# Order of the 512-column and the 256-column matmul in alternate weight tiles of a decoder block

## The chip, the cores and the metric

The kernel runs on one core of one Trainium2 chip, as one program of 20,150 profiled instructions. The metric is the device time of one execution in microseconds. The core has five engines with their own instruction streams: TensorE (PE in the profile; its weight loads are shown apart, as PEld), VectorE (DVE), ScalarE (ACT), GpSimd (POOL) and SyncE (SP), which issues most of the DMAs.

## What is computed

One layer of a decoder for 256 tokens of width 2048, in float32: a mixer with 16 heads of three kinds, cross attention with four heads over a memory of 256 tokens, and an MLP of width 8192, each with a residual and an RMS norm.

```python
h = rms_norm(x, g_mix)
qkv = h @ w_in                          # 2048 x 6144
merged = concat(rms_norm(moba(q, k, v)), rms_norm(stick_breaking(q, k, v)),
                rms_norm(dilated_mixture(q, k, v)))
x = x + merged @ w_out                  # 1536 x 2048
x = x + cross_attention(rms_norm(x), rms_norm(mem), w_cq, w_ckv, w_co)
u = rms_norm(x) @ w_up                  # 2048 x 8192
x = x + square(relu(u)) @ w_down        # 8192 x 2048
return rms_norm(x, g_final)
```

## The kernel before

Every product of the reference with a weight matrix is done in two parts, high and low. A float32 operand is split into a `float32r` value (`high`) and the rest (`low`), and a product is the sum of three: high by high, high by low, and low by high. ScalarE makes the high part of the weights (`w_high`, a copy, line 364), VectorE the low part (`w_low`, a subtraction, line 673). The activations stand in `part_a` or `part_b` as `[128, tile, 2, 256]`: for each tile of 128 rows of the contraction the high part and behind it the low part, for 256 tokens.

The weights come in jobs of 1 MB (`staged`, four buffers). A job has 16 weight tiles of 128 x 128. `w_high` and `w_low` each hold two jobs. TensorE takes a job in two halves of 8 tiles (`half_job`, line 1004). Ahead of a half it waits until VectorE has counted `low_ready` for it, and with the last matmul of a half it counts `half_done`, on which ScalarE waits before it splits the same half of the job after next into the same place.

Most jobs are *wide*. For a wide tile TensorE issues two matmuls. The one here called W has the high weights as its stationary operand and all 512 columns of the tile (high and low activations together) as its moving operand, and writes all 512 columns of a PSUM bank. The one called L has the low weights and the 256 high columns, and adds into the bank's first 256 columns. After the job the bank's two halves are added: VectorE and ScalarE do that while TensorE is in the next jobs (there are four banks). The first tile of a bank has to begin with W, since only W covers the whole bank and clears it (line 1020); the other tiles have L first (line 1021) and W second (line 1023).

The wide jobs are: 12 jobs of the q and k projections for the stick-breaking heads (one job for one bank of 16 tiles), 8 jobs of the output projection (two banks of 8 tiles each), 4 jobs of the cross attention's query, and the 128 jobs of the MLP. The MLP goes in four quarters, each with 16 jobs `up` and 16 jobs `down`. The `down` jobs read `part_b`, which holds the quarter's 16 tiles of squared activations. Before tiles 0, 8, 12 and 15 of its first job, `down` waits for `hid_low`, which VectorE counts when such a tile is ready (line 961).

The rest of the jobs use other forms: the value projections with matmuls of 512 columns only (lines 1066 to 1068), and the rotary heads, the memory keys, part of the output projection and the cross output with three matmuls of 256 columns for a tile (lines 1025 to 1027). All run in the order in which they are written; no scheduler moves anything.

Of the kernel before, what the change touches and what calls it, by code (L numbers as in the profile page):

```python
# [86 lines left out]
def build(nc, x_in, mem_in, wqk_in, wv_in, wmk_in, wmv_in, wbc_in, woa_in, wcq_in, wco_in,  # L87
# [4 lines left out]
    with ExitStack() as ctx:  # L92
# [908 lines left out]
        def _(pe):  # L1001
            mm = nc.tensor.matmul

            def half_job(off, job, half, out, part, tiles, count=8, total=KT, place=0, wide=True,
                         slot=lambda kt: kt, waits={}):

                pe.wait_ge(low_ready, off(2) + (2 * job + half + 1))
                for n in range(count):  # L1010
                    if n in waits:
                        pe.wait_ge(*waits[n])
                    kt = tiles + n
                    cols = slice(half * HALF + (place + n) * P, half * HALF + (place + n + 1) * P)
                    high, low = w_high[:, job % 2, cols], w_low[:, job % 2, cols]
                    first, last_tile = kt == 0, kt == total - 1
                    if wide:
                        both = part[:, slot(kt), :, :].rearrange("p a n -> p (a n)")
                        if first:
                            mm(out[:, :], high, both, start=True, stop=False)  # L1020
                        last = mm(out[:, 0:T], low, part[:, slot(kt), 0, :], start=False, stop=False)  # L1021
                        if not first:
                            last = mm(out[:, :], high, both, start=False, stop=last_tile)  # L1023
                    else:
                        mm(out[:, 0:T], high, part[:, slot(kt), 0, :], start=first, stop=False)  # L1025
                        mm(out[:, 0:T], high, part[:, slot(kt), 1, :], start=False, stop=False)  # L1026
                        last = mm(out[:, 0:T], low, part[:, slot(kt), 0, :], start=False, stop=last_tile)  # L1027
                return last

            def job_of(off, job, n_out, part, ready=None, wide=True, slot=lambda kt: kt):  # L1030

                pe.wait_ge(taken, off(1) + (n_out + 1))
                for half in range(2):
                    waits = {}
                    if ready is not None:

                        waits = ({0: (ready, 12), 4: (ready, 14), 6: (ready, KT)} if half
                                 else {0: (ready, 8)})
                    half_job(off, job, half, bank[job % 4], part, 8 * half, wide=wide,
                             slot=slot, waits=waits).then_inc(half_done, 1)  # L1040

            def short_jobs(job, n_out, part, at, waits={}):

                for s in range(4):
                    for half in range(2):
                        for t in (2 * half, 2 * half + 1):
                            pe.wait_ge(taken, n_out + 4 * s + t + 1)
                            last = half_job(none, job + s, half, bank[t], part, 0, 4, 4,
                                            place=4 * (t % 2), wide=False, slot=lambda kt: at + kt,
                                            waits={} if s or t else waits)  # L1050
                        last.then_inc(half_done, 1)
# [95 lines left out]
            with pe.Fori(0, HEADS_A // 2) as i:  # L1147
                for s in range(4):
                    job_of(by(i), JOB_A + s, OUT_A + s, part_a, wide=False)
                    if s == 0:  # L1150
                        pe.wait_ge(held_ready, i * 6 + (3 * 4 + 6))
                        pe.wait_ge(o_taken, i + (1 + HEADS_B))
                        for g in range(3):
# [3 lines left out]
                                      start=True, stop=True)  # L1157
# [42 lines left out]
            for s in range(8):  # L1200
                for half in range(2):
                    t = 2 * s + half
                    pe.wait_ge(taken, OUT_BC + t + 1)
                    pe.wait_ge(merged_low, 8)
                    half_job(none, JOB_BC + s, half, bank[t % 4], part_a, 0, 8, 8).then_inc(half_done, 1)
                if s < 4:
                    group_a(1, s)
                if s == 5:
                    norm_sum(N_A, extra[3])
# [164 lines left out]
```

## Time and profile before

| what | value |
|---|---|
| time, median of 3 runs | 1224.55 us (1224.54 to 1224.73) |
| span of the profiled execution | 1222.6 us |
| PE busy | 1205.0 us (99%), 7164 matmuls |
| PE weight loads busy | 1063.4 us (87%) |
| VectorE busy | 797.6 us (65%) |
| ScalarE busy | 605.1 us (49%) |
| GpSimd busy | 172.4 us (14%) |
| DMA | 224.25 MB, 183 GB/s over the span |
| chain of work that ended last | PE 92%, DVE 5%, the rest 3% |

Matmuls are pipelined, so that one starts long before the record of the one ahead ends. The duration in a matmul's row is therefore not what it costs. Its cost in a stream is the distance from its start to the start of the next. The start times in the timeline have a resolution of 0.01 us, so that a price of a few nanoseconds is read over many matmuls, or over several places of the same kind.

### The profile page before, as it was taken

Reading aid. Unit: us, or ns where it says so; the run is one execution under the profiler, and the core shown is the slowest. Engines: PE = TensorE matmul, PEld = TensorE weight load, DVE = VectorE, ACT = ScalarE, POOL = GpSimd, SP = SyncE. Lnnn points to the kernel's source line nnn. Section 1 sums busy time; section 2 is a strip of 40 time slices with the busy share of each in tenths; the row PEclk is TensorE's granted clock in tenths of the full one; section 3 lists DMA queues with packets and bytes.
Section 4 is the critical chain, followed back from the end, with each engine's and each line's share of the span. In section 5 each row is a group of like instructions: output and inputs, shape, how many; then the busy total and the mean of one; then the engine's idle time right before and its main releaser. Section 6 shows DMA issues by size and latency. Waiting matters only on the chain.

```text
span 1222.6 us, 20150 instructions
## 1 busy us (share of the span) xinstructions
PE 1205.0 (99%) x7164; PEld 1063.4 (87%) x7164; DVE 797.6 (65%) x1085; ACT 605.1 (49%) x897; POOL 172.4 (14%) x176
## 2 busy tenths in 40 slices
PE   8999999999999999999999999999999999999996
PEld 6888899999989889888888888888888888888885
DVE  8658766786668858666555666655666555666554
ACT  6345445555645656555433555333555333555442
POOL 8206500030323405000000000000000000000342
PEclk9999999999999999999999999999999999999998
DMA  9674543443644544455554455545555555455531
GB/s 357 213 269 174 201 177 138 144 166 137 242 172 169 177 153 155 151 196 186 196 199 174 172 191 187 206 172 197 172 180 183 197 197 177 172 186 196 200 138 69
DMA packets 33011, 224.25 MB, mean 183 GB/s; under 512 B 3793, under 2 KB 4177, under 8 KB 7121
## 3 DMA queue, kind: packets, MB, share of 16 engines
q1 hardware_dynamic: 32256, 220.22, 50.3%
q10 hardware_dynamic: 720, 3.59, 0.8%
q8 instruction: 21, 0.34, 0.1%
q14 instruction: 14, 0.11, 0.0%
HBM read 221.69 MB, written 2.10 MB: 183 GB/s over the span
## 4 chain that ended last, share of the span: by engine, by line
PE 92%; DVE 5%; ACT 1%; POOL 1%; issue 1%; DMA 0%; DVEq 0%; SPq 0%; ACTq 0%; POOLq 0%
PE bank L1023 43%; PE bank L1021 23%; PE bank L1025 4%; PE bank L1027 4%; PE bank L1026 4%; PE bank L1020 3%; PE bank L1066 2%; PE bank L1067 2%; PE bank L1068 2%; DVE w_low L673 2%; DVE part_a L718 1%; DVE part_a L883 1%; PE extra L1083 1%; POOL acc L302 0%; ACT w_high L364 0%
## 5 line engine op out<-in xcount | busy, mean ns | idle before, releaser
L673 DVE TENSOR_TENSOR w_low<-staged,w_high 128x1024 fp32r<-128x1024 f32 x407 | 508.5, 1264 | 215.6 <-ACT w_high L364 210.7
L364 ACT ACTIVATE w_high<-staged 128x1024 fp32r<-128x1024 f32 x400 | 415.0, 1054 | 338.2 <-PE bank L1023 244.8
L1023 PE MATMUL bank<-part_a,w_high 128*128 128x512 f32 x1312 | 467.7, 398 | 0.0
L1021 PE MATMUL bank<-part_a,w_low 128*128 128x256 f32 x1408 | 379.6, 281 | 0.0
L1023 PE MATMUL bank<-part_b,w_high 128*128 128x512 f32 x960 | 342.4, 399 | 0.0
L1023 PEld LDWEIGHTS bank<-part_a,w_high 128*128 128x128 f32 x1312 | 246.5, 188 | 56.8
L1021 PE MATMUL bank<-part_b,w_low 128*128 128x256 f32 x1024 | 277.2, 281 | 0.0
L1021 PEld LDWEIGHTS bank<-part_a,w_low 128*128 128x128 f32 x1408 | 266.0, 189 | 7.9
L1023 PEld LDWEIGHTS bank<-part_b,w_high 128*128 128x128 f32 x960 | 180.4, 188 | 42.0
L1021 PEld LDWEIGHTS bank<-part_b,w_low 128*128 128x128 f32 x1024 | 193.5, 189 | 5.5
L293 POOL TENSOR_TENSOR squares<-x 128x256 f32<-128x256 f32 (+1 forms) x31 | 35.0, 1130 | 683.3 <-DVE x L971 678.7
L1025 PE MATMUL bank<-part_a,w_high 128*128 128x256 f32 x384 | 110.1, 287 | 0.1
L1027 PE MATMUL bank<-part_a,w_low 128*128 128x256 f32 x384 | 108.7, 283 | 0.0
L1026 PE MATMUL bank<-part_a,w_high 128*128 128x256 f32 x384 | 108.6, 283 | 0.0
L961 DVE TENSOR_TENSOR part_b<-spare,part_b 128x256 f32 x64 | 27.2, 425 | 79.8 <-ACT part_b L633 79.8
L1025 PEld LDWEIGHTS bank<-part_a,w_high 128*128 128x128 f32 x384 | 73.7, 192 | 0.5 <-POOL part_a L307 0.4
L1026 PEld LDWEIGHTS bank<-part_a,w_high 128*128 128x128 f32 x384 | 73.6, 192 | 0.1
L1027 PEld LDWEIGHTS bank<-part_a,w_low 128*128 128x128 f32 x384 | 73.6, 192 | 0.0
L628 ACT ACTIVATE spare<-bank 128x256 f32<-128x256 f32 x64 | 24.5, 383 | 85.9 <-PE bank L1023 85.9
L295 POOL TENSOR_TENSOR acc<-acc,squares 128x256 f32<-128x256 f32 x59 | 59.7, 1011 | 4.6
L631 ACT ACTIVATE spare<-spare 128x256 f32<-128x256 f32 x64 | 26.7, 418 | 65.5 <-DVE spare L957 65.5
L969 DVE TENSOR_TENSOR x<-x,bank 128x256 f32 (+1 forms) x64 | 26.9, 421 | 46.1 <-PE bank L1023 45.9
(153 smaller groups left out, 1162.2 us busy)
## 6 DMA issues: line engine op xcount, KB each, us to landing
staged<-in_wup SPq DMA_DIRECT2D x64, 1024.0 KB, 4.8
staged<-in_wdown SPq DMA_DIRECT2D x64, 1024.0 KB, 4.7
staged<-in_wqk SPq DMA_DIRECT2D x32, 1024.0 KB, 4.8
staged<-in_wv SPq DMA_DIRECT2D x12, 1024.0 KB, 4.9
staged<-in_wbc SPq DMA_DIRECT2D x8, 1024.0 KB, 5.0
staged<-in_wmk SPq DMA_DIRECT2D x4, 1024.0 KB, 4.8
staged<-in_woa SPq DMA_DIRECT2D x4, 1024.0 KB, 4.8
staged<-in_wcq SPq DMA_DIRECT2D x4, 1024.0 KB, 4.9
```

The costliest lines, as they stand in the source:

```text
L293: nc.gpsimd.tensor_tensor(squares[:, 0, :], tile, tile, ALU.mult).then_inc(sq_made, 1)
L295: nc.gpsimd.tensor_tensor(acc[:, :], acc[:, :], squares[:, 0, :], ALU.add).then_inc(acc_made, 1)
L364: nc.scalar.activation(w_high[:, job % 2, cols], staged[:, job % 4, cols], ACT.Copy).then_inc(high_ready, 1)
L673: tt(w_low[:, job % 2, cols], staged[:, job % 4, cols], f32(w_high[:, job % 2, cols]), ALU.subtract).then_inc(low_ready, 1)
L961: tt(part_b[:, i * 4 + s, 1, :], spare[:, 1, :], f32(part_b[:, i * 4 + s, 0, :]), ALU.subtract).then_inc(hid_low, 1)
L969: tt(x[:, i * 4 + s, :], x[:, i * 4 + s, :], bank[s][:, 0:T], ALU.add).then_inc(x_wide, 1)
L1020: mm(out[:, :], high, both, start=True, stop=False)
L1021: last = mm(out[:, 0:T], low, part[:, slot(kt), 0, :], start=False, stop=False)
L1023: last = mm(out[:, :], high, both, start=False, stop=last_tile)
L1025: mm(out[:, 0:T], high, part[:, slot(kt), 0, :], start=first, stop=False)
L1026: mm(out[:, 0:T], high, part[:, slot(kt), 1, :], start=False, stop=False)
L1027: last = mm(out[:, 0:T], low, part[:, slot(kt), 0, :], start=False, stop=last_tile)
```

## The change

In wide tiles the order of the two matmuls now depends on the tile's number: tiles with an even number have W first and L second, tiles with an odd number L first and W second. Before, tile 0 had W first and all others L first. The operands, the number of matmuls and the waits stay as they are. The flag that clears the bank is on W of tile 0 as before.

```diff
                     if wide:
                         both = part[:, slot(kt), :, :].rearrange("p a n -> p (a n)")
-                        if first:
-                            mm(out[:, :], high, both, start=True, stop=False)
+                        if kt % 2 == 0:
+                            mm(out[:, :], high, both, start=first, stop=False)
                         last = mm(out[:, 0:T], low, part[:, slot(kt), 0, :], start=False, stop=False)
-                        if not first:
+                        if kt % 2:
                             last = mm(out[:, :], high, both, start=False, stop=last_tile)
```

The first place is on TensorE, at the start of a 16-tile job of the q and k projections: `bank1` is the job's PSUM bank, L1020 and L1023 are the two lines of W, L1021 is L. Before, from the first tile on:

```order
L1009 REGISTER_ALU
L1020 MATMUL bank1<-part_a,w_high 128x512
L1021 MATMUL bank1<-part_a,w_low 128x256 x2
L1023 MATMUL bank1<-part_a,w_high 128x512
L1021 MATMUL bank1<-part_a,w_low 128x256
L1023 MATMUL bank1<-part_a,w_high 128x512
```

With the change:

```order
L1009 REGISTER_ALU
L1020 MATMUL bank1<-part_a,w_high 128x512
L1021 MATMUL bank1<-part_a,w_low 128x256 x2
L1023 MATMUL bank1<-part_a,w_high 128x512
L1020 MATMUL bank1<-part_a,w_high 128x512
L1021 MATMUL bank1<-part_a,w_low 128x256 x2
L1023 MATMUL bank1<-part_a,w_high 128x512
```

The four matmuls that already opened the job (W, L, L, W) now repeat for each two tiles, where L and W had alternated.

The second place is on TensorE too, in the output projection with its banks of 8 tiles, behind six transposes of the attention. Before:

```order
L1094 MATMUL extra<-square,values 128x128 x6
L1020 MATMUL bank<-part_a,w_high 128x512
L1021 MATMUL bank<-part_a,w_low 128x256 x2
L1023 MATMUL bank<-part_a,w_high 128x512
L1021 MATMUL bank<-part_a,w_low 128x256
L1023 MATMUL bank<-part_a,w_high 128x512
```

With the change:

```order
L1094 MATMUL extra<-square,values 128x128 x6
L1020 MATMUL bank<-part_a,w_high 128x512
L1021 MATMUL bank<-part_a,w_low 128x256 x2
L1023 MATMUL bank<-part_a,w_high 128x512
L1020 MATMUL bank<-part_a,w_high 128x512
L1021 MATMUL bank<-part_a,w_low 128x256 x2
```

Here, too, the first two tiles stay, and the third one's W has moved ahead of its L. On the other engines no instruction moves.

## Rows read from the trace of the kernel before

**Rows 1.** The page: the span, and the TensorE clock granted in 40 slices.

```profile
span 1222.6 us, 20150 instructions
...
PEclk9999999999999999999999999999999999999998
```

**Rows 2.** Waits of PE: line, waited for, us in total, times, longest.

```profile
PE bank L1066 <- DVE w_low L673: 2.8, 6, 1.6
PE extra L1075 <- POOL acc L302: 1.9, 2, 1.1
```

**Rows 3.** Busy time by stretch: us, then us and count of each engine, clock, DMA.

```profile
101.00:168.00 67.00, 67.00 (x381) 58.21 (x381) 53.78 (x62) 35.58 (x51) 35.26 (x33) 1.00 0.49 179
...
500.00:1211.00 711.00, 711.00 (x4032) 617.60 (x4031) 434.91 (x567) 335.38 (x455) 33.63 (x30) 1.00 0.51 180
```

**Rows 4.** Timeline of PE from one up job's start to the next: start, duration.

```profile
702.72 0.40 PE L1023 MATMUL bank<-part_a,w_high 128*128 128x512 f32 x1
702.96 0.39 PE L1020 MATMUL bank<-part_a,w_high 128*128 128x512 f32 x1
703.18 0.40 PE L1021 MATMUL bank<-part_a,w_low 128*128 128x256 f32 x2
703.42 0.40 PE L1023 MATMUL bank<-part_a,w_high 128*128 128x512 f32 x1
703.65 0.28 PE L1021 MATMUL bank<-part_a,w_low 128*128 128x256 f32 x1
703.77 0.40 PE L1023 MATMUL bank<-part_a,w_high 128*128 128x512 f32 x1
704.01 0.28 PE L1021 MATMUL bank<-part_a,w_low 128*128 128x256 f32 x1
...
708.60 0.39 PE L1020 MATMUL bank<-part_a,w_high 128*128 128x512 f32 x1
...
709.30 0.28 PE L1021 MATMUL bank<-part_a,w_low 128*128 128x256 f32 x1
```

**Rows 5.** The same timeline from 703.5 us, where only the second L is left.

```profile
703.30 0.28 PE L1021 MATMUL bank<-part_a,w_low 128*128 128x256 f32 x1
```

**Rows 6.** PE in the value projections, first and last of 19 matmuls.

```profile
61.76 0.39 PE L1068 MATMUL bank<-w_high,part_a 128*128 128x512 f32 x1
...
65.84 0.39 PE L1068 MATMUL bank<-w_high,part_a 128*128 128x512 f32 x1
```

**Rows 7.** PE in jobs of three 256-column matmuls, first and last of 36.

```profile
388.73 0.28 PE L1026 MATMUL bank<-part_a,w_high 128*128 128x256 f32 x1
...
392.93 0.28 PE L1025 MATMUL bank<-part_a,w_high 128*128 128x256 f32 x1
```

**Rows 8.** PE at the start of the first down stage and of the second up stage.

```profile
578.73 0.39 PE L1020 MATMUL bank<-part_b,w_high 128*128 128x512 f32 x1
...
579.42 0.28 PE L1021 MATMUL bank<-part_b,w_low 128*128 128x256 f32 x1
...
669.08 0.39 PE L1020 MATMUL bank<-part_a,w_high 128*128 128x512 f32 x1
```

**Rows 9.** The lines L1020 and L1021 alone: count, duration min/median/max, first and last start.

```profile
L1020 PE MATMUL bank<-part_a,w_high x96: 389/389/585, 100.9 to 1115.2; 128*128 128x512 f32 x96
...
L1020 PE MATMUL bank<-part_b,w_high x64: 389/389/389, 578.7 to 1205.5; 128*128 128x512 f32 x64
...
L1021 PE MATMUL bank<-part_a,w_low x1408: 274/281/285, 101.2 to 1120.5; 128*128 128x256 f32 x176
...
L1021 PE MATMUL bank<-part_b,w_low x1024: 277/281/284, 579.0 to 1210.8; 128*128 128x256 f32 x171
```

**Rows 10.** Timeline: last hidden tile ready on DVE, and its first use by PE.

```profile
581.56 0.42 DVE L961 TENSOR_TENSOR part_b<-spare,part_b 128x256 f32 x1 [1.26 <-ACT part_b L633]
...
584.02 0.28 PE L1021 MATMUL bank<-part_b,w_low 128*128 128x256 f32 x1
```

**Rows 11.** Timeline around the output projection's end: ACT, POOL and PE.

```profile
376.16 1.06 ACT L364 ACTIVATE w_high<-staged 128x1024 fp32r<-128x1024 f32 x1 [2.24 <-PE bank L1023]
...
382.19 2.31 POOL L307 TENSOR_TENSOR part_a<-spare,part_a 128x256 fp32r<-128x256 f32 x2 [0.81 <-ACT part_a L503]
...
384.55 0.39 PE L1025 MATMUL bank<-part_a,w_high 128*128 128x256 f32 x1
```

## The prediction, made before the changed kernel had run

> **What bounds the kernel now.** I read the page's head first, then the waits of PE, then the busy times by stretch, and last the starts in PE's timeline one by one. The granted clock is at the full 2.4 GHz from the first slice to the last [rows 1], so nothing here is about the clock. PE waits for other engines for a few us in all: 2.8 us for low weights in the first 32 us, 1.9 us for GpSimd's sums before two norms [rows 2]. In the stretches of the wide jobs it never stands still: 67.00 us busy in 67, and 711.00 in 711 through the MLP, where VectorE is busy 434.91 and ScalarE 335.38 [rows 3]. So in these stretches the time is the number of matmuls times the distance between their starts. The busy share can't show whether such a distance is as short as it could be; the starts can.
>
> **What a pair of matmuls costs, by its neighbours.** I call the 512-column matmul W and the 256-column one L. In an up job [rows 4] the first four starts are W 702.96, L 703.18, L 703.30 [rows 5], W 703.42, and the next tile's L is at 703.65. From there L and W alternate for 14 tiles until the next job's W at 708.60: 4.95 us / 14 = 353.6 ns for a tile, 707 ns for two. One such tile shows the parts: L 703.65 to W 703.77 is 0.12, W 703.77 to L 704.01 is 0.24. The first two tiles of the job, with the same two W and two L but in the order W L L W, take 703.65 - 702.96 = 0.69 us. The same distance is 0.70 one job later [rows 4] and 579.42 - 578.73 = 0.69 in a down job [rows 8]. As a cross-check, a whole job takes (669.08 - 578.73) / 16 = 5.647 us [rows 8]; less 14 x 0.3536 = 4.950 this leaves 0.697. So W L L W costs 0.690 to 0.697 where L W L W costs 0.707.
>
> Two other stages tell the same without mixing lengths. Where every matmul has 512 columns, 18 distances take 65.84 - 61.76 = 4.08 us, or 226.7 ns each [rows 6]. Where every matmul has 256, 35 distances take 392.93 - 388.73 = 4.20 us, or 120.0 ns each [rows 7]. Two of each make 2 x (226.7 + 120.0) = 693 ns. That is the price of W L L W, and not that of the alternation, which costs 14 ns more. An order with equal neighbours thus costs what the pure streams cost, and each return from W to L in the alternation is dearer: a W that follows an L takes 0.236 or so, one that follows a W takes 0.22 to 0.23 (702.96 to 703.18). Why that is I can't read from the records, and the sum doesn't need it.
>
> **The change part by part.** It removes no matmul and adds none. It turns each two tiles that read L W L W into W L L W, except the first two of each bank, which have that order already. How many are there? L1021 counts 1408 + 1024 = 2432 wide tiles, L1020 counts 96 + 64 = 160 banks [rows 9]. Of the 160, 144 banks have 16 tiles (12 + 4 + 128 jobs) and 16 have 8: 144 x 16 + 16 x 8 = 2432, which agrees. Two tiles of each bank are as before, so 144 x 7 + 16 x 3 = 1056 groups of four matmuls change their order.
>
> The saving for a group is 707.2 - 693 = 14.2 ns by the pure streams, and 707.2 - 692.5 = 14.7 by the mean of the job starts at 0.69, 0.69 and 0.70. One thing in the new order has no row: in it the second W of a group is followed by another W, where at the job start it is followed by an L. The nearest row is the last W of a job, followed by the next job's W: 702.96 - 702.72 = 0.24, no dearer than the alternation's. I take 14.5 ns. 1056 x 14.5 = 15.3 us.
>
> What of this is not on the path? At three places a chain on other engines ends the stage, and TensorE gets to the wait earlier without gaining. At the end of the output projection, PE goes on at 384.55, right as GpSimd's second subtraction ends (382.19 + 2.31 = 384.50), a chain that begins with ScalarE's split at 376.16 [rows 11]. In these 8.4 us stand some 9 changed groups, whose 9 x 14.5 = 0.13 us is lost. The two waits for GpSimd's sums [rows 2] come each behind one wide job of 7 groups, the first of the cross query and the first of the MLP: 2 x 7 x 14.5 ns = 0.2 us lost. That leaves 15.3 - 0.3 = 15.0 us.
>
> What would be late next? The weights: ScalarE and VectorE have to split each job in 5.54 us where they had 5.65. VectorE is busy 434.91 / 711 = 61% of the MLP and 53.78 / 67 = 80% of the q and k stage [rows 3]. 2% less time makes that 62% and 82%, and PE waits for neither now. The hidden activations: the last tile of a quarter is ready at 581.56 + 0.42 = 581.98, and down uses it first at 584.02 [rows 10], with 2.04 us to spare. Seven groups in between shorten that by 0.1. The banks, and the count at a half's end, stand where they stood: the last matmul of each half is W of an odd tile before and after. The loads follow VectorE's splits and run at half the DMA engines' share [rows 3]. So I cost all of these at nothing.
>
> The profiled execution: 1222.6 - 15.0 = 1207.6 us. The median of the runs shown stands 1.95 us above the span, which the change doesn't touch: **1209.5 us**.
>
> **The bounds.** A W behind a pair of L and ahead of a W has no row, so I bound it from both sides. At best it takes the 226.7 ns of the pure stream, where the job start has it at about 0.233 (703.42 to 703.65): 1056 x 6 ns = 6 us less, 1203.5. At worst it takes the 0.236 of the alternation: 1056 x 3 ns = 3 us more, 1212.7. I hold the upper end, with a us for reading errors of 1 ns in a group, at 1214, and the lower at 1205, since the row nearest to the case (0.233) speaks against the whole of the gain.
>
> **Rivals.** First, *no change*: the short distance belongs to the start of a bank. There W clears the bank in place of adding to it, and it goes to another bank than the W before. Inside a bank W would then cost 0.236 whatever stands ahead of it. What remains is a few ns at most: 1224.5, and not below 1222. For it speaks that my row of a W behind a W in mixed jobs is always at such a start. Against it: in rows 6 nearly every matmul adds (line 1066 clears only at tile 0), three in a row go to the same bank, and the mean is still 226.7. I give it 6 in 100. The Trainium skill (TensorE: Matmul & The Clock Gate, section Back-to-back issue gap) has a rule that leads to the same end: the distance of warm matmuls is their columns / 2.4 plus some 2.5 ns, with no word on the neighbours. By that rule W costs 216 and L 109 ns in either order, and this change gives nothing. The trace does not agree with it: 226.7 and 120.0 in the pure streams, and 0.24 for W in the alternation. What the rule lacks is just what is at issue.
>
> Second, *half of it*: the cheap W (0.22 against 0.24) needs a new bank, but the two L next to each other, with their common 0.24 for the two (703.18 to 703.42), and the W behind them keep their price. Then a group costs about 0.701 in place of 0.693, the saving is 6 ns, and the time 1224.55 - 1056 x 6 ns = 1218.2. For and against it stand the same rows. I give it 5 in 100.
>
> Third, *slower*: two W in one bank disturb each other. The second W starts to add to column 0 of the bank 0.23 us after the first, while the record of the first lasts 0.39 to 0.40 us [rows 4]. In the old order an L stands between two W of a bank, except where the bank changes. If the second had to wait for the first one's record to end, it would cost 0.17 us in each of 1056 groups, 180 us in all. It decides from 14.5 ns a group. Against it: rows 6 have three such matmuls in a row in one bank at 226.7 ns, and the two L at the job's start overlap in the same way. A weak form, of 30 ns a group, would give 1224.5 + 1056 x 15.5 ns = 1241. 2 in 100.
>
> **How the numbers follow.** The forecast has 87 in 100, no change 6, half of it 5, slower 2. The range for 8 in 10 is that of the forecast alone, 1205 to 1214. About 0.2% (2.4 us) is what a measurement of this kernel can tell from no change. Faster by more: 87 + 5 and a little of the rest, 0.92. Within: 0.06. Slower: 0.02.
>
> **What would show it.** In the changed kernel's timeline two tiles in the middle of an up job should take 0.69 us where now they take 0.707, a whole job 5.54 in place of 5.65, and the stages with matmuls of one length should stay at 226.7 and 120.0 ns. The sum is right if the span falls by 15 us, about 13 of them between the MLP's begin and its end. The waits of PE should show no new line in the MLP. Wrong would be: W behind W inside a bank at 0.24 (first or second rival) or more (third), or a new wait for VectorE's low weights.

## The result and the profile after

The changed kernel takes 1214.47 us (median of 4 runs, 1214.26 to 1214.81), the kernel before 1224.58 beside it. The ratio is 0.9917, with a 95% interval of 0.9904 to 0.9931. So it is faster by 10.1 us, where 15.0 were forecast: the direction is right, and the time lies half a microsecond above the stated range.

The page of the changed kernel, its head and the granted clock, against [rows 1], and the waits of PE, against [rows 2]:

```profile
span 1212.5 us, 20150 instructions
...
PEclk9999999999999999999999999999999999999999
```

```profile
PE bank L1066 <- DVE w_low L673: 2.6, 5, 1.6
PE extra L1075 <- POOL acc L302: 2.0, 2, 1.1
```

The busy times by stretch, against [rows 3] (stretch, then us and count of PE, weight loads, VectorE, ScalarE, GpSimd; clock; DMA share and GB/s):

```profile
101.00:168.00 67.00, 67.00 (x387) 58.53 (x388) 55.09 (x64) 35.91 (x51) 35.16 (x33) 1.00 0.51 182
500.00:1200.00 700.00, 700.00 (x4021) 611.09 (x4020) 434.34 (x566) 334.50 (x454) 33.58 (x30) 1.00 0.51 183
```

The clock is at its upper level as before and PE is still busy without a gap. The waits are those of before but for one: in the first 20 us, ahead of every changed instruction, PE also waits 1.1 us for low weights of another line (L724), 0.9 us more for low weights in all. Nothing new bounds the wide stages, and the whole gain lies in the distances of the starts. The timeline of PE at the start of the first down stage, and at the start of the second up stage 16 jobs later, against [rows 8]:

```profile
576.86 0.39 PE L1020 MATMUL bank<-part_b,w_high 128*128 128x512 f32 x1
577.09 0.40 PE L1021 MATMUL bank<-part_b,w_low 128*128 128x256 f32 x2
577.33 0.40 PE L1023 MATMUL bank<-part_b,w_high 128*128 128x512 f32 x1
577.56 0.40 PE L1020 MATMUL bank<-part_b,w_high 128*128 128x512 f32 x1
577.79 0.39 PE L1021 MATMUL bank<-part_b,w_low 128*128 128x256 f32 x2
578.02 0.40 PE L1023 MATMUL bank<-part_b,w_high 128*128 128x512 f32 x1
578.26 0.39 PE L1020 MATMUL bank<-part_b,w_high 128*128 128x512 f32 x1
...
666.03 0.39 PE L1020 MATMUL bank<-part_a,w_high 128*128 128x512 f32 x1
```

A job takes (666.03 - 576.86) / 16 = 5.573 us, where it took 5.647 and 5.54 was forecast. Two tiles take (578.26 - 576.86) / 2 = 0.70 us, not 0.69. From here on I give distances in nanoseconds, taken from the start times in the trace. They repeat to a nanosecond or two. L118 is an L whose follower starts 118 ns after it. The two kernels in the middle of an up job read:

```
before   L118 W241  L120 W236  L113 W232 | L118 W241  L120 W236  L113 W232 | ...    1060 for 3 tiles, 353.3 each
after    W231 L113  L120 W233  W236 L116  L112 W233 | W231 L112 ...                 1393.3 for 4 tiles, 348.3 each
```

Where the 10.1 us lie can be read by comparing when each stage begins in the two traces. The middle column is the prediction's sum, split by its own counts of groups (84, 48, 28 and 896, at 14.5 ns) and its own losses:

| stretch | gain in the sum, us | gain measured, us |
|---|---|---|
| up to the first wide job | 0 | -0.32 |
| q and k | 1.22 | 0.88 |
| output projection | 0.57 | 0.08 |
| cross query | 0.30 | 0.12 |
| MLP | 12.89 | 9.31 (127 jobs x 73.3 ns) |

The first wide job begins 0.32 us later in the changed kernel. That shift is there by 16 us, where no instruction differs, and goes from run to run: in the traces of this study that job begins between 100.84 and 101.58 us.

### The profile page after: what moved, and what is told of

It is laid out like the page before. It is cut to its first block, busy times and chain, and to the rows that moved or that the text cites. A ratio compares the mean times of both kernels' runs of the same rounds, so it can differ in the third digit from the quotient of the medians.

```text
span 1212.5 us, 20150 instructions
## 1 busy us (share of the span) xinstructions
PE 1193.7 (98%) x7164; PEld 1057.0 (87%) x7164; DVE 797.9 (66%) x1085; ACT 605.0 (50%) x897; POOL 172.4 (14%) x176
## 4 chain that ended last, share of the span: by engine, by line
PE 92%; DVE 5%; ACT 1%; POOL 1%; issue 1%; DMA 0%; DVEq 0%; SPq 0%; ACTq 0%; POOLq 0%
PE bank L1023 23%; PE bank L1020 23%; PE bank L1021 23%; PE bank L1025 4%; PE bank L1027 4%; PE bank L1026 4%; PE bank L1066 3%; PE bank L1067 2%; PE bank L1068 2%; DVE w_low L673 2%; DVE part_a L718 1%; DVE part_a L883 1%; PE extra L1083 1%; DMA staged<-in_wv 0%; POOL acc L302 0%
## 5 line engine op out<-in xcount | busy, mean ns | idle before, releaser
L1021 PEld LDWEIGHTS bank<-part_a,w_low 128*128 128x128 f32 x1408 | 264.7, 188 | 61.9
L1020 PE MATMUL bank<-part_a,w_high 128*128 128x512 f32 x704 | 279.7, 397 | 0.0
L1023 PE MATMUL bank<-part_a,w_high 128*128 128x512 f32 x704 | 278.5, 396 | 0.0
L1021 PE MATMUL bank<-part_a,w_low 128*128 128x256 f32 x1408 | 276.6, 278 | 0.0
L1021 PEld LDWEIGHTS bank<-part_b,w_low 128*128 128x128 f32 x1024 | 192.5, 188 | 45.3
L1023 PE MATMUL bank<-part_b,w_high 128*128 128x512 f32 x512 | 202.5, 396 | 0.0
L1020 PE MATMUL bank<-part_b,w_high 128*128 128x512 f32 x512 | 202.3, 395 | 0.0
L1021 PE MATMUL bank<-part_b,w_low 128*128 128x256 f32 x1024 | 201.1, 278 | 0.0
L1020 PEld LDWEIGHTS bank<-part_a,w_high 128*128 128x128 f32 x704 | 133.7, 190 | 0.2
L1023 PEld LDWEIGHTS bank<-part_a,w_high 128*128 128x128 f32 x704 | 131.9, 187 | 0.0
L1027 PE MATMUL bank<-part_a,w_low 128*128 128x256 f32 x384 | 108.7, 283 | 0.0
L1020 PEld LDWEIGHTS bank<-part_b,w_high 128*128 128x128 f32 x512 | 97.2, 190 | 0.0
L1023 PEld LDWEIGHTS bank<-part_b,w_high 128*128 128x128 f32 x512 | 95.9, 187 | 0.0
L1025 PEld LDWEIGHTS bank<-part_a,w_high 128*128 128x128 f32 x384 | 73.7, 192 | 0.5 <-POOL part_a L307 0.4
L1026 PEld LDWEIGHTS bank<-part_a,w_high 128*128 128x128 f32 x384 | 73.7, 192 | 0.1
```

The source lines that it names most:

```text
L1020: mm(out[:, :], high, both, start=first, stop=False)
```

## The experiments

The diffs in this section are abridged, but for the first; a comment in them stands for lines that are left out. Jobs are timed from the first matmul of one to the first of the next.

### Alternation from the first tile to the last

My first theory (A) was the prediction's: each matmul has a price by its neighbours. The rival (B) came from a second look at the trace of before. There the alternation L W does not have one price. In the output projection seven of the 16 banks of 8 tiles read 233, 117, 231, 112 from their third tile on, that is 346.7 ns for a tile, and two more go at this price in their later tiles; so does one of the cross query's four jobs. Two banks in a row, in steps and by their first matmuls:

```
before, 345.6   W236 L116 L112 W233  L117 W231 L112 W233  L117 W231 L113 W232  L118 W231 ...   346.7 a tile
before, 348.3   W230 L114 L119 W233  L118 W241 L120 W235  L114 W232 L118 W241  L120 W235 ...   353.3 a tile
```

```profile
345.56 0.40 PE L1020 MATMUL bank<-part_a,w_high 128*128 128x512 f32 x1
348.34 0.39 PE L1020 MATMUL bank<-part_a,w_high 128*128 128x512 f32 x1
351.16 0.40 PE L1020 MATMUL bank<-part_a,w_high 128*128 128x512 f32 x1
```

The first bank takes 2.78 us, the second, with the same matmuls in the same order, 2.82. So there are two steady rhythms, which I call the fast one (346.7 ns a tile) and the slow one (353.3). The kernel of this run never has two of a kind side by side:

```diff
-                        if first:
-                            mm(out[:, :], high, both, start=True, stop=False)
-                        last = mm(out[:, 0:T], low, part[:, slot(kt), 0, :], start=False, stop=False)
-                        if not first:
-                            last = mm(out[:, :], high, both, start=False, stop=last_tile)
+                        mm(out[:, :], high, both, start=first, stop=False)
+                        last = mm(out[:, 0:T], low, part[:, slot(kt), 0, :], start=False, stop=last_tile)
```

> In every wide tile W (512 columns) stands ahead of L (256), so that the two alternate from the first tile to the last and nowhere two of a kind meet. Theory A (the price of a matmul hangs on its neighbours: each change between lengths costs some ns, two of a kind side by side save it): 353.7 ns for a tile everywhere, no cheap start of a job, 5.65 us for a job or a little more, about 1225.5 us. Theory B (the starts fall into one of two steady rhythms, 346.7 or 353.3 ns for a tile of alternating matmuls, both seen in the kernel before; which one holds is set by the steps at a job's start, and the two L side by side there bring the slow one back): with no such pair the rhythm of the first job stays, 5.547 us a job and about 1210.5 us if it is the fast one, 5.653 us a job and 1225.5 if it is the slow one, and it may change only where another stage comes in between.

Measured: ten runs, and they form two groups with nothing between. Four lie at 1211.81, 1212.29, 1212.35 and 1212.37 us, six from 1225.04 to 1226.14 (a mean ratio of 0.9970, 0.9936 to 1.0005, says nothing of either). The trace was of the first kind. The first matmul of its first down stage and of its second up stage:

```profile
577.97 0.39 PE L1019 MATMUL bank<-part_b,w_high 128*128 128x512 f32 x1
...
666.71 0.39 PE L1019 MATMUL bank<-part_a,w_high 128*128 128x512 f32 x1
```

(666.71 - 577.97) / 16 = 5.546 us a job, the pure price (832 x 6.667 ns). In the same trace the q and k stage has the slow rhythm; two matmuls in it that are ten jobs apart:

```profile
107.29 0.40 PE L1019 MATMUL bank<-part_a,w_high 128*128 128x512 f32 x1
...
163.82 0.40 PE L1019 MATMUL bank<-part_a,w_high 128*128 128x512 f32 x1
```

(163.82 - 107.29) / 10 = 5.653 us a job. Theory A, with one price for one order, can explain neither the two groups nor the two stages. The distance between the groups, 13.3 us by their means, is near the 127 jobs x 106.7 ns = 13.5 us that the rhythms ask for.

> The kernel with W ahead of L in every wide tile once more, for a second trace of it: its ten times fell into two groups, four at 1211.8 to 1212.4 us and six at 1225.0 to 1226.1, and the trace was taken of the first kind (5546.5 ns for each MLP job). Rhythm theory: a run of the other kind has 5653 ns for each MLP job from the first to the last, never a mixture; the difference of 106.7 ns x 127 = 13.5 us is that of the two groups. If it is of the first kind again the MLP jobs read 5547. Against it: prices in between, or a change in the middle of the MLP.

Measured: 1212.15 us in one run, MLP jobs of 5547 ns again, the q and k stage slow again. No trace shows this kernel in its other group; a slow MLP with this order is shown by the last kernel below. Both traces have the first MLP job in the slow rhythm and all later ones in the fast. Between the first and the second PE waits for GpSimd's sum for the norm, 1.08 us in both, here in the first one's trace:

```profile
494.23 0.70 PE L1072 MATMUL extra<-acc,square 128*128 128x256 f32 x2 [1.08 <-POOL acc L302]
```

Behind that pause the rhythm is another. So a pause can be where one run parts from the next; that it was so in the runs at 1225 us is not shown.

### Longer stretches of one kind

```diff
-                for n in range(count):
+                for n in range(0, count, 4):      # tiles n to n + 3
+                    # W of the four tiles, then their L; in every second group L first
```

> Each half of 8 wide tiles has four W, eight L and four W, so that the lengths change twice in a half where the changed kernel has them change four times and the kernel before some 15 times. The waits for a tile's activations stand ahead of its group of four. Theory A (changes of length cost): the changed kernel's excess over the pure streams (5.573 - 5.547 = 0.027 us a job) halves, 5.56 us a job, about 1212.5 us. Theory B (rhythms): long runs pin each length to its pure price, 226.7 and 120.0 ns, 5.547 us a job, about 1210.7 us; a price above the changed kernel's would speak against both.

Measured: 1216.09 us (4 runs, ratio 0.9930, 0.9911 to 0.9946), 5587 ns a job. Both theories expected less than the changed kernel's 5573, and both missed. (The changed kernel changes lengths eight times in a half, not four as the expectation has it; theory A should have said 5553, and missed by more.) The steps show a price that neither had:

```
runs of four   L120 L120 L120  W233 W236 W228 W233 W231 W226 W227 W227  L113 L119 L120 L120 ...
```

Behind a stretch of L the next five W cost 233, 236, 228, 233 and 231 where the pure price is 226.7, together 27 ns more. The first L behind a stretch of W costs 113 in place of 120. A return costs 20 ns in all, there are two in a job, and 5547 + 40 = 5587.

> W x8, L x8 in the first half of a job, L x8, W x8 in the second, so that a job has one stretch of 16 W (across the job's border) and one of 16 L. Per-change theory as the runs of four read: a change from a long stretch of L to W costs 20 ns over the pure prices, spread over the next five W, and one from W to L nothing: 5546.7 + 20 = 5567 ns a job, 0.9 us less than the changed kernel over 144 jobs, about 1213.6, plus the waits: the activations' counts now stand ahead of a whole half, and the first down job of a quarter asks for tile 15 some 0.4 us before it is ready (4 x 0.4 = 1.8 us) and the first jobs after a norm likewise: about 1215.5 us. If the length of a stretch doesn't matter, 5587 a job as with the runs of four and 1218.

Measured: 5567 ns a job, as worked out from that price, but 1217.19 us (4 runs, 0.9939, 0.9923 to 0.9956). The waits of PE in this kernel, in its line numbers (L1020 is L):

```profile
PE bank L1020 <- DVE part_a L883: 2.9, 2, 1.5
...
PE bank L1020 <- DVE part_b L961: 1.7, 4, 0.5
```

The four waits for the hidden activations cost 1.7 us, where 1.8 were expected; those behind the two norms cost 2.9, more than I had put down. So a price that was read from one kernel's steps foretold another's job to the nanosecond, though not its waits.

### Which side the dear steps come from

```diff
-                        last = mm(out[:, 0:T], low, part[:, slot(kt), 0, :], start=False, stop=False)
+                        last = mm(low_out[:, 0:T], low, part[:, slot(kt), 0, :],   # extra[2] in the MLP
+                                  start=first, stop=last_tile)
```

> The order of the kernel before, but in the MLP's 128 jobs L writes into another PSUM bank (extra2) than W, so that no two neighbours touch the same bank; the low part is left out of the sums, which leaves the number of matmuls and the work of the other engines as they are. If the dear steps come from two matmuls that add into the same columns one right behind the other, a tile falls from 353.7 to 346.7 ns, the job to 5.55 us, about 1212 us. If they come from the sides of weights and moving columns, or from a rhythm of the starts, nothing changes: 5.647 us a job and 1224.5 us.

Measured: 1224.66 us in one run, 5647 ns a job, and the steps of the kernel before (L117 W241 L120 W236 L113 W233). Two neighbours that add into the same bank are not the cause.

```diff
-                        last = mm(out[:, 0:T], low, part[:, slot(kt), 0, :], start=False, stop=False)
+                        last = mm(out[:, 0:2 * T], low, both, start=False, stop=False)   # MLP only
```

> In the MLP's 128 jobs L moves 512 columns too, so that the low weights meet the low activations as well (work that the kernel before leaves out), in the order of the kernel before. If the pure price that the prediction took from the value projections holds where the weights are the stationary operand, every step is 226.7 ns, a tile 453.3 and a job 7253 ns: 128 x 1607 ns = 205.6 us more, about 1430 us. If W costs more in this place (233, as most W of the changed kernel), a job is near 7460 ns and the time 1456.

Measured: 1428.81 us, in one run. The first matmul of the first down stage and of the second up stage:

```profile
603.22 0.39 PE L1020 MATMUL bank<-part_b,w_high 128*128 128x512 f32 x1
...
719.27 0.39 PE L1020 MATMUL bank<-part_a,w_high 128*128 128x512 f32 x1
```

(719.27 - 603.22) / 16 = 7.253 us a job. The pure price of [rows 6] holds here as well, 32 x 226.7 ns. The steps there are 225 to 228 ns throughout. This stream of one length shows no rhythm; the extra nanoseconds came with the mixture.

### Where the two places stand that have two of a kind

```diff
-                        if first:
+                        if kt < heads:          # heads: 16, 7, 8, 5 in up, 16, 1, 4, 11 in down
                             mm(out[:, :], high, both, start=first, stop=False)
                         last = mm(out[:, 0:T], low, part[:, slot(kt), 0, :], start=False, stop=False)
-                        if not first:
+                        if kt >= heads:
                             last = mm(out[:, :], high, both, start=False, stop=last_tile)
```

> In the MLP the first n tiles of a job have W first and the rest L first, with n = 16, 7, 8, 5 for the four jobs of an up loop and 16, 1, 4, 11 for those of a down loop (the kernel before has n = 1 everywhere). Each job with n under 16 has one place with two L side by side and one with two W. Rhythm theory: between such places the distance is 346.7 or 353.3 ns for a tile and nothing else, the places are where it changes, and which one follows depends on how many tiles stand between, so that jobs of one loop differ among themselves by up to 100 ns but repeat from loop to loop. Neighbour theory: all jobs with n under 16 cost 5647 as before, those with n = 16 5660, whatever n is.

Measured: 1220.22 us, in one run. From the second job of the first down stage on, with n = 1, 4, 11, 16, the jobs cost 5647, 5646, 5631, 5554, then 5551, 5651, 5631, 5554 ns, and so on in that loop. The job with n = 1, the order of the kernel before, costs 5647 the first time and 5551 the three times after, and so in each of the four down stages. Its first matmul and that of the next job, the first time and the second:

```profile
584.52 0.40 PE L1020 MATMUL bank<-part_b,w_high 128*128 128x512 f32 x1
590.17 0.39 PE L1020 MATMUL bank<-part_b,w_high 128*128 128x512 f32 x1
...
607.00 0.39 PE L1020 MATMUL bank<-part_b,w_high 128*128 128x512 f32 x1
612.55 0.39 PE L1020 MATMUL bank<-part_b,w_high 128*128 128x512 f32 x1
```

5.65 us and 5.55: one order, two prices, by what ran before it. In the up loop n = 16, 7, 8, 5 cost 5644, 5647, 5631 and 5558; the neighbour theory had 5660 and 5647.

> As the kernel before, but each job of 16 tiles has its first n tiles with W first and the rest with L first, with n = 4 in the 12 jobs of the q and k stage, 2 in the up jobs and 8 in the down jobs (the kernel before has n = 1). The matmuls and the number of places with two of a kind side by side (two in a job) are those of the kernel before. Neighbour theory: each n costs 5647 ns a job, 1224.5 us. Rhythm theory: the price of n is its own, between 5551 (fast between the two places) and 5650 (slow), the same from job to job once it has settled. In the traces so far the fast rhythm has a period of two tiles and went over to the slow one where two W met after an odd count of tiles with L first; with an even n that count is even (12, 14 or 8), so that fast may follow fast: then 5.55 us in the MLP and about 1211 us.

> The same with n = 6 in the q and k stage, 12 in the up jobs and 7 in the down jobs. Neighbour theory: 5647 ns everywhere, 1224.5 us. Rhythm theory: again a price for each n between 5551 and 5650; if even counts let the fast rhythm stay, n = 6 and 12 are near 5551 and n = 7 is not, and a quarter of the MLP (16 up, 16 down) costs some 1.5 us less than before.

Measured, in one run each: 1218.43 us with n = 4, 2, 8 and 1222.74 with n = 6, 12, 7. The neighbour theory's 5647 for every n is wrong. But the other expectation holds only in part: most n settle at a price of their own, n = 2 and 8 never settle at one, n = 12 has two, and the even-odd rule is wrong:

| tiles with W first | ns a job, once settled |
|---|---|
| 1 (kernel before) | 5647 |
| 2, 8 | 5560 and 5633 in turn |
| 4 | 5647 |
| 6 | 5593 |
| 7 (down jobs) | 5647 |
| 12 | 5627, from the second quarter on 5633 |

What these traces gave was a list of steps. The fast rhythm comes in two forms, 230, 117 in each tile or 233, 117, 231, 112 in two. The slow one goes 241, 120, 236, 113, 233, 117 in three tiles (5650, 5650 and 5660 ns for 16 tiles, in turn). Two of a kind side by side lead from one to the other, and which way depends on the step at which they meet. Two L behind a slow "W233 L117" lead on as 121, 238, 117, 236, 116, 224, 117, 234, 117, 241. Two W behind a slow 241 lead to 238 and then to 230, 117 for good.

### One job that decides 126

If that list is right, an order of matmuls in one job has to set the time of all that follow. The MLP alternates throughout with W first; the other stages have the changed kernel's order; only the second of the 128 MLP jobs differs, and differently in the two kernels:

```diff
+            def up(off, s, ready=None, order="WL" * 8):       # of a half; down has it too
             for s in range(4):
-                up(none, s, x2_low if s == 0 else None)
+                # fast: first half "W" * 8 + "L" * 8, second "WL" + "LW" * 5 + "WL" * 2
+                # slow: first half "W" * 8 + "L" * 8, second "WL" * 8
+                up(none, s, x2_low if s == 0 else None, one_job if s == 1 else "WL" * 8)
```

> All MLP jobs alternate with W first (W L W L), as in the kernel of the first run, and the other stages have the changed kernel's order; only the MLP's second job differs: W x8, L x8, then W L, five tiles with L first and two with W first. By the steps of the traces so far the eight L wipe out what was before, the alternation behind them is slow and reads 234, 117 (one tile), two L side by side bring 121, 238, 117, 236, 116, 224, 117, 234, 117, 241, and two W side by side right behind the 241 bring 238 and then the fast rhythm of 230 and 117. Rhythm theory: each of the 126 MLP jobs behind it costs 5547 ns in every run, 26.7 ns less than in the changed kernel, 3.4 us in all: 1211.1 us, with no second group of times at 1225. If the steps hang on something else than the order of the matmuls, the times fall into two groups again, or lie at 1224.5.

> The same kernel, but the MLP's second job has W x8, L x8 and then eight tiles with W first, without the two places that lead to the fast rhythm. The same matmuls in the same order in the 126 jobs behind it. Rhythm theory: the slow rhythm holds from there to the end in every run, 5653 ns a job, 126 x 106.7 ns = 13.4 us more than its neighbour: 1224.5 us. Neighbour theory, or any in which a job's cost comes from its own order: both kernels within 0.2 us of each other.

Measured: 1210.95 us with the fast job (4 runs, 1210.65 to 1211.05; ratio 0.9890, 0.9873 to 0.9906) and 1224.63 with the slow one (10 runs, 1224.06 to 1224.88; ratio 0.9999, 0.9990 to 1.0009). Neither has a second group of times. The fast one's timeline at that job's end, with the two W side by side at 497.63:

```profile
497.17 0.28 PE L1023 MATMUL bank<-part_a,w_low 128*128 128x256 f32 x1
497.28 0.40 PE L1021 MATMUL bank<-part_a,w_high 128*128 128x512 f32 x1
497.52 0.28 PE L1023 MATMUL bank<-part_a,w_low 128*128 128x256 f32 x1
497.63 0.64 PE L1021 MATMUL bank<-part_a,w_high 128*128 128x512 f32 x2
498.11 0.28 PE L1023 MATMUL bank<-part_a,w_low 128*128 128x256 f32 x1
498.23 0.39 PE L1021 MATMUL bank<-part_a,w_high 128*128 128x512 f32 x1
498.46 0.28 PE L1023 MATMUL bank<-part_a,w_low 128*128 128x256 f32 x1
498.57 0.39 PE L1021 MATMUL bank<-part_a,w_high 128*128 128x512 f32 x1
```

The times in these rows are too coarse to tell 346.7 from 353.3; the steps tell them apart. From the two L side by side on they are:

```
L117 L121 W238 L117 W236 L116 W224 L118 W233 L117 W241 W238 L116 W230 L117 | W230 L117 W230 L116 ...
```

These are the steps that had been expected, to the nanosecond or two to which they repeat, and behind the two W (241 and 238, together the 0.48 us from 497.63 to 498.11) comes the fast rhythm, and it stays. In the slow kernel the second half of that job reads W233 L118 W241 L120 W236 L113 W232 L118, and this stays too. The same two starts, 16 jobs apart, in the fast kernel and in the slow one:

```profile
576.23 0.39 PE L1021 MATMUL bank<-part_b,w_high 128*128 128x512 f32 x1
...
664.98 0.39 PE L1021 MATMUL bank<-part_a,w_high 128*128 128x512 f32 x1
```

```profile
578.41 0.40 PE L1021 MATMUL bank<-part_b,w_high 128*128 128x512 f32 x1
...
668.87 0.40 PE L1021 MATMUL bank<-part_a,w_high 128*128 128x512 f32 x1
```

88.75 / 16 = 5.547 us against 90.46 / 16 = 5.654. The matmuls between these starts, their order, their operands and their waits are the same in both. Of the 13.7 us between the two kernels, 13.4 lie in the 126 jobs behind the one that differs, up to 700 us after it. This settles that the price is not in an order alone but in the rhythm that a stream is in, and that the rhythm can be set. The fast kernel is 3.5 us faster than the changed one, and the fastest of this study.

## Why the prediction missed

- **What bounds the kernel, and what would be late next.** Right. PE's starts were the bound before and after, VectorE, the hidden tiles and the loads never became one, and no new wait appeared in the MLP.
- **The count of 1056 groups.** Right as a count. But the groups of the output projection were not all of the dear kind: about half of its banks were already in the fast rhythm. In a slow bank the change saves some 29 ns (2816 to 2787), in a fast one it costs 9 (2777 to 2786). The stage gave 0.08 us, where 0.57 were in the sum. I had read the alternation's price in the MLP alone and had taken it for the price everywhere. The cross query has one such job of four.
- **The two jobs whose gain would be lost.** Right: the first job of the cross query takes 6.99 and 6.98 us up to the next, the first of the MLP 7.24 in both kernels.
- **The price of the alternation, 353.6 ns a tile.** Right for the MLP of that kernel, and wrong as the price of that order: it has a second one, 346.7, in the same trace.
- **The price of W L L W, 692.5 to 693 ns.** This step failed, and it carries most of the miss. "An order with equal neighbours thus costs what the pure streams cost" does not hold: the group costs 696.7 in the changed kernel. The saving in the MLP is therefore 10.5 ns a group and not 14.5, and that makes 3.6 us there and 0.3 in the q and k stage, 3.9 of the missing 4.9. The output projection lacks another 0.5 and the cross query 0.2, where the saving was taken from jobs that had been in the fast rhythm. The last 0.3 are the later start, which has nothing to do with the change. The W of tile 0, 0.22 to 0.23 us in [rows 4], stood behind a slow stretch, and its 226.7 ns were a step on the way from one rhythm to the next. In the steady order the W behind a W costs 230.8 and 235.8 in turn. Two ways of reading 693 agreed by chance: the job start's first four steps, and the sum of the pure streams, which is the fast rhythm's price and not this order's.
- **The bound for the W without a row.** The range was made from this one step, the W that closes a group and has another W behind it, at 227 to 236. The averages over 60 down jobs put it at 232.6 to 233.4, inside. The matmul that went wrong was the other one, the W that opens a group, which I had thought to know: 226.7 at the job start of before, 233.3 on average now. The two L give 2 ns of that back. For this step the range held nothing, and so it was half a microsecond too short.
- **The rivals.** "No change", since the short step would belong to a new bank, is wrong: in the changed kernel W costs 230.8 at tile 0 and 230.7, 230.8 and 230.8 at tiles 4, 8 and 12, which are in the same bank as the W before. "Half of it" came nearest in its time (1218.2), though not by its reason. Two W in one bank did not hold each other up as the third rival had it: the second starts 231 to 236 ns after the first, where that rival had some 0.4 us.
- **The Trainium skill's rule** (TensorE: Matmul & The Clock Gate, section Back-to-back issue gap), columns / 2.4 + 2.5 ns, would have had no change; the runs show 226.7 in place of 216 for 512 columns, and besides that up to 6.7 ns more a tile by the rhythm. The same section calls this the gap of an isolated matmul, which the prediction left out, and gives 131 ns for a matmul of 512 columns in a stream with weight loads. No run here shows such a price: the streams of 512 columns go at 226.7.

So the mechanism is shown as far as this: the price hangs on the rhythm that the stream is in, and the saving was sized from four steps on the way between two rhythms. Open is what in TensorE makes the rhythms. The runs exclude the shared bank, the clearing of a bank and the length of W by itself. Whether the weight loads or the reading of the moving columns lie behind it was not tried. In the MLP's traces the loads start 1 to 6 ns behind a matmul, and that distance goes with the rhythm: 2 or 3 ns throughout where each tile reads 230, 117, and up to 5 in the slow one. The traces don't show which of the two follows the other.

## What to carry to other kernels

A price taken from the first steps of a pattern is not the pattern's price: take it from a stretch in which the steps repeat, and look for a second stretch of the same order elsewhere in the trace before multiplying it by a thousand. Where a stream of matmuls of two lengths bounds a kernel, list the distances from start to start and find the period. If the same order shows two periods, look at what runs ahead of it: here one job in another order was worth 13.4 us over the 126 behind it, more than the order of all the others had given. And where a kernel's times fall into two groups, as those of the kernel that only alternates did, such a stream is one thing to look for.

## What the runs showed of the hardware

- Alternating matmuls of 512 and 256 columns (`float32r`, each with its own 128 x 128 weights, clock at its upper level) go at 346.7 or at 353.3 ns for a pair, steadily for 700 us, with nothing but the past to tell them apart (the kernels with one job changed). The times of one kernel that only alternates fell into two groups from run to run, 1212 and 1225 us, which fits; only the first was traced.
- Streams of one length go at 226.7 ns (512 columns) and 120.0 (256). A return from a stretch of 8 or 16 matmuls of 256 columns to 512 costs 20 ns for the round: 27 more over five matmuls of 512, and 7 less at the first of 256 behind them.
- Averaged over its period, a steady job of 16 tiles took a whole number of steps of 6.667 ns: 832 in the fast rhythm, 835 and 838 with runs of eight and four, 836 in the changed kernel, 847 before, 848 in the slow rhythm, 1088 with 512 columns throughout. Single jobs need not: in the slow rhythm they take 5650, 5650 and 5660 ns in turn.
